# Pooling mixer of an encoder trunk: turned input from memory, row factors by a product with ones, pooled product in the mix banks

## The chip, the cores and the metric

The kernel runs on one core of one Trainium2 chip. The metric is the device time of one execution in microseconds. The core has the matrix engine TensorE (PE in the profile), VectorE (DVE), ScalarE (ACT), GpSimd (POOL) and the queue of SyncE (SP), which only issues transfers here.

## What is computed

One layer (DEPTH is 1) over 2048 rows of a prompt and 512 rows of a sample, each row 1024 wide, all in float32. Cut to what matters:

```python
def rms_norm(x, g):
    y = xf * lax.rsqrt(jnp.mean(xf * xf, axis=-1, keepdims=True) + EPS)
    return y * g

def pool_mixer(h, w, scale):                  # windows 2, 4, 8, 16 rows, 256 channels each
    mean = (take(cs, t + win // 2) - take(cs, t - win // 2)) / cnt
    d = stack(mean - h)                       # per group of 256 channels
    return einsum('bsgc,gce->bsge', d, w) * scale

x = x + pool_mixer(rms_norm(x, norm_mix_g), pool_w, pool_scale)
x = x + sqrelu_mlp(rms_norm(x, norm_mlp_g), w_up, w_down)     # 1024 -> 4096 -> 1024
return rms_norm(x, final_norm_g)
```

## The kernel before

The 2560 rows are five groups of 512 rows. A group goes through the MLP in eight steps (`PAIRS`), so there are 40 steps `n`, with `g = n // 8` and `s = n % 8`. A step has four up tiles (`up_tile`: 24 matmuls of 512 columns each) and the seven products of a Strassen scheme for the down projection (`product`, P1, P5, P6, P3, P4, P7, P2 in this order, 12 matmuls of 512 columns each) of the step before. Each float32 operand is split into a high and a low part (`*_hi`, `*_lo`): ScalarE makes the high part, VectorE the low one. The products go into a ring of two bank pairs (`ring_ps`, turn numbers in `TURN`); VectorE adds each pair into `m_acc` (`evict`). In the steps of group 0 the parts of the down weights are made as well (`split_w`, `sum_w` on VectorE, `w_slot`) and stored; later groups load them again.

While group `g` is in the MLP, the pooling of group `g + 1` is done beside it. In step `s` = 2 (`STATS_STEP`) its rows are loaded to `xr`, ScalarE sums squares (`row_stats`), and GpSimd makes the factor of each row, `rs_x`. In each of the steps 3 to 6 one window `w` of 256 channels is done (16 times in all). ScalarE scales the rows (`norm_rows`, in the step before). TensorE turns them, 8 transposes at the start of the step (`turn_window`) and 2 for the rows beyond the group's ends after the second product (`turn_halos`), into the two banks of `mix_ps`. ScalarE copies them to `ht`. GpSimd sums neighbours in `w + 1` levels (`window_sums`), VectorE subtracts the rows themselves, ScalarE and VectorE split (`dt_hi`, `dt_lo`), and TensorE multiplies by the pooling weights (`pool_out`, 24 matmuls of 256 columns, in two halves, each a turn of the ring). VectorE adds that to `xr` (`add_pooled`).

The order on each engine is written out by hand, engine by engine, in that engine's `step(n)` and `boundary(n)`; semaphores order the engines against each other. What an engine does in an instruction it does not begin before the one ahead of it in this order. The order on TensorE in a window's step is: `turn_window`, up tile 0, P1, P5, `turn_halos`, up tile 1, P6, P3, up tile 2, P4, P7, `pool_out`, up tile 3, P2.

Two places in VectorE's `step(n)` matter below: the part after P7's eviction, which prepares the down weights and activations of the next step (`sum_w`, `split_w`, `split_a`, then `sum_a(n, P5)`, `evict(q0 + P2)`, `split_a(q0 + NP + P5)`); and the end of the step `s` = 2. Group 0 runs from 40 to 394 us of the span, step 2 of it ends at 145.1 us.

Of the kernel before, what the change touches and what calls it, by code (L numbers as in the profile page):

```python
# [6 lines left out]
P = 128  # L7
D = 1024
# [15 lines left out]
TURNS = CT + 1  # L24
# [57 lines left out]
def ring_turns():  # L82

    turns, at = {}, 0
    for n in range(STEPS + 1):
        for k in range(NP if n > 0 else 0):
            turns[NP * (n - 1) + k] = at
            at += 1
            if k == P7 and n < STEPS and pooled_window(n) is not None:
                for half in range(2):  # L90
                    turns[(*pooled_window(n), half)] = at
                    at += 1
    return turns
# [23 lines left out]
def build(nc, x, halos, w_up, w_down, pool_w, pool_scale, g_mix, g_mlp, g_fin, ends, bands, ident_in,  # L117
# [8 lines left out]
    with ctx:  # L126
# [69 lines left out]

        junk = dt_hi[:, :, :].rearrange("p c t -> p (c t)")
# [88 lines left out]
        p4_begun = sem("p4_begun")  # L286
        first_full = sem("first_full")
# [21 lines left out]
        xw_done = sem("xw_done")  # L309
        x_turned = sem("x_turned")  # L310
        ht_done = sem("ht_done")
# [27 lines left out]
        def window_sums(engine, eng, w, ht, room, done_sem, done):  # L339
            src = ht  # L340
# [16 lines left out]
        def _(sp):  # L357
# [38 lines left out]
            def load_halos(m):  # L396
                if m > 1:
                    sp.wait_ge(xw_done, NORMS * WINDOWS * (m - 1))
                sp.dma_start(xh[:, :], halos[m]).then_inc(halo_in, 16)

            def load_pool_w(m, w):
                before = (m, w - 1) if w > 0 else (m - 1, WINDOWS - 1)
                if (*before, 1) in TURN:
                    sp.wait_ge(ring_full, TURN[(*before, 1)] + 1)
# [33 lines left out]
            def step(n):  # L438
# [3 lines left out]
                if mixes and s == STATS_STEP:  # L442
# [4 lines left out]
                    load_ends(g + 1)  # L447
                    load_pool_w(g + 1, 0)
# [32 lines left out]
        def _(act):  # L481
# [932 lines left out]
```

## Time and profile before

| | before |
|---|---|
| median of 3 runs | 1790.6 us (1790.18 to 1791.56) |
| the profiled execution | 1790.22 us, its span 1788.4 us |
| granted clock, mean share | 0.996 |
| PE busy | 1756.3 us (98%) |
| DVE, ACT, POOL busy | 1122.7 (63%), 761.4 (43%), 158.7 us (9%) |
| DMA | 432.67 MB, mean 242 GB/s |

A time in a row of the trace is counted from the start of the span. "Busy" merges overlapping instructions: matmuls overlap, so the spacing of their starts says more than their durations.

### The profile page before, as it was taken

To read this page: it belongs to the slowest core of one execution; us is meant where nothing else is said; L and a number is where in the kernel's file an instruction comes from. 1 tells how busy PE (TensorE), PEld (TensorE's weight loads), DVE (VectorE), ACT (ScalarE), POOL (GpSimd) and SP (SyncE) were. 2 spreads that over 40 slices of the span, in tenths; PEclk is the share of its full clock that TensorE was granted. 3 is DMA by queue.
4 is the path that set the end of the run, shared out by engine and by line. 5 is a ranking of instruction groups with operands and counts; after the bars stand their busy time and mean duration, and the time that the engine had idled before them with its cause. 6 is when DMAs were issued, how large, how long until landed. Compare 5 with 4: busy or idle time off the path is not lost.

```text
span 1788.4 us, 20968 instructions
## 1 busy us (share of the span) xinstructions
PE 1756.3 (98%) x8156; PEld 1461.8 (82%) x8156; DVE 1122.7 (63%) x1178; ACT 761.4 (43%) x1186; POOL 158.7 (9%) x139
## 2 busy tenths in 40 slices
PE   8999999999999999999999999999999999999996
PEld 8888887778888888888888888888888888888885
DVE  6678888786555564765555647645556575445447
ACT  6556554554343335344333344343333543233232
POOL 4000112001001120010011200000112010000001
PEclk9999999999999999999999999999999999999998
DMA  7597766668856665668666555776665657666654
GB/s 266 218 348 281 265 252 242 245 263 326 307 212 224 223 224 212 247 242 295 243 223 223 213 212 204 280 295 223 224 224 212 235 205 273 240 223 239 233 202 163
DMA packets 80902, 432.67 MB, mean 242 GB/s; under 512 B 8860, under 2 KB 10780, under 8 KB 42916
## 3 DMA queue, kind: packets, MB, share of 16 engines
q1 hardware_dynamic: 57764, 347.44, 52.6%
q10 hardware_dynamic: 23040, 83.90, 13.8%
q8 instruction: 65, 1.06, 0.2%
q14 instruction: 33, 0.27, 0.0%
HBM read 360.00 MB, written 71.30 MB: 241 GB/s over the span
## 4 chain that ended last, share of the span: by engine, by line
PE 89%; DVE 6%; ACT 1%; DMA 1%; issue 1%; POOL 1%; ACTq 0%; SPq 0%; POOLq 0%; DVEq 0%
PE up_ps L1169 16%; PE up_ps L1171 16%; PE up_ps L1170 16%; PE ring_ps L1188 13%; PE ring_ps L1190 13%; PE ring_ps L1189 13%; DVE m_acc L832 1%; PE ring_ps L1213 1%; DVE w_slot L765 1%; PE ring_ps L1215 1%; PE ring_ps L1214 1%; DVE a_slot L773 1%; PE mix_ps L1198 1%; DVE wu_lo L756 1%; DMA wd_raw<-w_down 1%
## 5 line engine op out<-in xcount | busy, mean ns | idle before, releaser
L756 DVE TENSOR_TENSOR wu_lo<-wu_raw,wu_hi 128x1024 fp32r<-128x1024 f32 x158 | 195.8, 1239 | 579.7 <-ACT wu_hi L496 579.7
L1169 PE MATMUL up_ps<-h_hi,wu_hi 128*128 128x512 f32 x1280 | 501.4, 392 | 0.6 <-DVE h_lo L897 0.6
L1171 PE MATMUL up_ps<-h_hi,wu_lo 128*128 128x512 f32 x1280 | 498.5, 389 | 0.0
L1170 PE MATMUL up_ps<-h_lo,wu_hi 128*128 128x512 f32 x1280 | 498.5, 389 | 0.0
L533 ACT ACTIVATE a_raw<-up_ps 128x512 f32<-128x512 f32 x160 | 95.3, 596 | 509.0 <-PE up_ps L1171 509.0
L832 DVE TENSOR_TENSOR m_acc<-ring_ps,m_acc 128x1024 f32<-128x1024 f32 x245 | 298.6, 1219 | 18.8 <-PE ring_ps L1190 18.4
L1188 PE MATMUL ring_ps<-w_slot,a_slot 128*128 128x512 f32 x760 | 296.8, 391 | 1.1 <-DVE m_acc L832 1.1
L1190 PE MATMUL ring_ps<-w_slot,a_slot 128*128 128x512 f32 x760 | 295.9, 389 | 0.0
L1189 PE MATMUL ring_ps<-w_slot,a_slot 128*128 128x512 f32 x760 | 295.7, 389 | 0.0
L1171 PEld LDWEIGHTS up_ps<-h_hi,wu_lo 128*128 128x128 f32 x1280 | 240.2, 188 | 50.5
L1169 PEld LDWEIGHTS up_ps<-h_hi,wu_hi 128*128 128x128 f32 x1280 | 240.3, 188 | 49.4 <-DVE h_lo L897 1.2
L1170 PEld LDWEIGHTS up_ps<-h_lo,wu_hi 128*128 128x128 f32 x1280 | 240.4, 188 | 48.3
L525 ACT CAST a_slot<-s_sum 128x512 fp32r<-128x512 f32 x160 | 99.4, 621 | 278.4 <-PE ring_ps L1190 98.5
L1188 PEld LDWEIGHTS ring_ps<-w_slot,a_slot 128*128 128x128 f32 x760 | 142.6, 188 | 31.1 <-issue 1.5
L1190 PEld LDWEIGHTS ring_ps<-w_slot,a_slot 128*128 128x128 f32 x760 | 142.6, 188 | 29.9
L1189 PEld LDWEIGHTS ring_ps<-w_slot,a_slot 128*128 128x128 f32 x760 | 142.7, 188 | 29.2
L496 ACT CAST wu_hi<-wu_raw 128x1024 fp32r<-128x1024 f32 x160 | 165.4, 1034 | 0.0
L1188 PE MATMUL ring_ps<-w_more,a_slot 128*128 128x512 f32 x360 | 140.6, 391 | 0.1
L1190 PE MATMUL ring_ps<-w_more,a_slot 128*128 128x512 f32 x360 | 140.2, 389 | 0.0
L1189 PE MATMUL ring_ps<-w_more,a_slot 128*128 128x512 f32 x360 | 140.1, 389 | 0.0
L773 DVE TENSOR_TENSOR a_slot<-s_sum,a_slot 128x512 fp32r<-128x512 f32 x160 | 134.1, 838 | 3.4 <-ACT a_slot L525 3.4
L525 ACT CAST a_slot<-a_raw 128x512 fp32r<-128x512 f32 x120 | 74.5, 621 | 104.6 <-PE ring_ps L1190 104.5
(136 smaller groups left out, 1642.2 us busy)
## 6 DMA issues: line engine op xcount, KB each, us to landing
w_slot<-w_cache SPq DMA_DIRECT2D x134, 1024.0 KB, 5.1
w_more<-w_cache SPq DMA_DIRECT2D x90, 1024.0 KB, 5.1
wu_raw<-w_up ACTq DMA_DIRECT2D x160, 512.0 KB, 3.2
w_cache<-w_slot SPq DMA_DIRECT2D x56, 1024.0 KB, 4.9
wd_raw<-w_down SPq DMA_DIRECT2D x16, 1024.0 KB, 8.7
xr<-x SPq DMA_DIRECT2D x20, 512.0 KB, 7.6
out<-m_acc SPq DMA_DIRECT2D x20, 512.0 KB, 5.6
pw_slot<-pw_cache SPq DMA_DIRECT2D x16, 512.0 KB, 4.3
```

The source lines that it names most:

```text
L496: nc.scalar.copy(wu_hi[:, u % FT, :, :], wu_raw[:, u % FT, :, :]).then_inc(wu_hi_done, 1)
L525: nc.scalar.copy(a_slot[:, q % A_SLOTS, 0, :, :], a_source(q)).then_inc(a_hi_done, 1)
L533: nc.scalar.activation(a, up_ps[:, u % FT, :], ACT.Relu).then_inc(relu_done, 1)
L756: nc.vector.tensor_tensor(wu_lo[:, u % FT, :, :], wu_raw[:, u % FT, :, :], wu_hi[:, u % FT, :, :].bitcast(f32), ALU.subtract).then_inc(wu_ ...
L773: nc.vector.tensor_tensor(a_slot[:, i, 1, :, :], a_source(q), a_slot[:, i, 0, :, :].bitcast(f32), ALU.subtract).then_inc(a_lo_done, 1)
L832: nc.vector.tensor_tensor(dst, src, dst, ALU.add).then_inc(ring_read, 1)
L1169: nc.tensor.matmul(o, hi, h2_hi[:, d, :], start=(d == 0), stop=False)
L1170: nc.tensor.matmul(o, hi, h2_lo[:, d, :], start=False, stop=False)
L1171: last = nc.tensor.matmul(o, lo, h2_hi[:, d, :], start=False, stop=(d == DT - 1))
L1188: nc.tensor.matmul(dst, a_hi, hi, start=(k == 0), stop=False)
L1189: nc.tensor.matmul(dst, a_hi, lo, start=False, stop=False)
L1190: last = nc.tensor.matmul(dst, a_lo, hi, start=False, stop=(k == 1))
```

## The change

- The input is given a second time, laid out with channels on partitions and with the rows beyond each group's ends (`x_turned`). Two slots `xt` take one window's channels each, by a transfer (`load_turned`, 128x1056 floats). The ten transposes of a window, the scaling in `norm_rows` and the copies to `ht` go.
- The row factors are spread over the partitions once a group. At the end of the step `s` = 2 VectorE sets a tile of ones and a tile with the factors on the diagonal (`set_diag`). At the start of step 3 TensorE multiplies them (`spread_rs`, four products of 128 columns and one of 16, in float32), and ScalarE copies the result to `rs_b` (`keep_rs`). GpSimd multiplies each slot by it, two instructions of 528 elements a window, ahead of the sums.
- The sums of window `w + 1` no longer wait for the transposes of the next step: they wait for the slot, for `rs_b`, and for `dt_lo` of window `w`.
- `pool_out` writes to the two banks of `mix_ps`, in one piece, and stands after up tile 3, behind which only P2 is left. `add_pooled` is one instruction, after the eviction of P2.
- On VectorE the window's subtraction and split stand after the eviction of P7; on ScalarE `split_pooled` stands after `split_a(q0 + 6)`.

```diff
             def load_halos(m):
                 if m > 1:
-                    sp.wait_ge(xw_done, NORMS * WINDOWS * (m - 1))
+                    sp.wait_ge(rs_spread, SPREADS * (m - 1))
+            def load_turned(m, w):
+                v = WINDOWS * (m - 1) + w
+                if v >= 2:
+                    sp.wait_ge(diff_done, v - 1)
+                sp.dma_start(xt[:, w % 2, :, :], x_turned[m - 1, w]).then_inc(xt_in[w % 2], 16)
...
                     load_ends(g + 1)
+                    load_turned(g + 1, 0)
+                    load_turned(g + 1, 1)
                     load_pool_w(g + 1, 0)
...
                 if mixes and WINDOW_STEP <= s < WINDOW_STEP + WINDOWS - 1:
                     load_pool_w(g + 1, s - WINDOW_STEP + 1)
+                if mixes and WINDOW_STEP <= s < WINDOW_STEP + WINDOWS - 2:
+                    load_turned(g + 1, s - WINDOW_STEP + 2)
...
+            def keep_rs(m):
+                act.wait_ge(rs_spread, SPREADS * m)
+                if m > 1:
+                    act.wait_ge(xt_scaled, CT * WINDOWS * (m - 1))
+                nc.scalar.copy(rs_b[:, HALO:HALO + GT], mix_ps[:, 0, :]).then_inc(rs_b_done, 1)
+                nc.scalar.copy(rs_b[:, 0:HALO], mix_ps[:, 1, 0:HALO]).then_inc(rs_b_done, 1)
+                nc.scalar.copy(rs_b[:, HALO + GT:HT], mix_ps[:, 1, HALO:2 * HALO]).then_inc(rs_b_done, 1)
...
             def add_pooled(m, w):
-                c = slice(w * WC, (w + 1) * WC)
-                for half in range(2):
-                    r = TURN[(m, w, half)]
-                    rows = xr[:, 2 * half:2 * half + 2, c]
-                    dve.wait_ge(ring_full, r + 1)
-                    nc.vector.tensor_tensor(rows, ring_pair(r)[:, :, 0:WC], rows, ALU.add).then_inc(ring_read, 1)
+                rows = xr[:, :, w * WC:(w + 1) * WC]
+                dve.wait_ge(pool_full, WINDOWS * (m - 1) + w + 1)
+                nc.vector.tensor_tensor(rows, mix_ps[:, :, :].rearrange("p b (i c) -> p (b i) c", c=WC), rows,
+                                        ALU.add).then_inc(pool_read, 1)
+
+            def set_diag(m):
+                dve.wait_ge(rs_x_done, m)
+                if m > 1:
+                    dve.wait_ge(rs_spread, SPREADS * (m - 1))
+                nc.vector.memset(ones, 1.0).then_inc(diag_done, 1)
+                nc.vector.tensor_tensor(rs_diag[:, 0:GT].rearrange("p (j t) -> p j t", t=P),
+                                        ident[:, :].unsqueeze(1).to_broadcast([P, TT, P]),
+                                        rs_x[:, 0:TT].unsqueeze(2).to_broadcast([P, TT, P]),
+                                        ALU.mult).then_inc(diag_done, 1)
+                nc.vector.tensor_scalar(rs_diag[:, GT:GT + 2 * HALO], ident[:, 0:2 * HALO], rs_x[:, TT:NORMS], None,
+                                        ALU.mult).then_inc(diag_done, 1)
...
-                if windows:
-                    subtract_own(g + 1, w)
-                    split_pooled(g + 1, w)
                 split_wu(4 * n + 4)
                 if n > 0:
                     evict(q0 + P4)
                     split_a(q0 + P2)
                     evict(q0 + P7)
+                if windows:
+                    subtract_own(g + 1, w)
+                    split_pooled(g + 1, w)
                 sum_w(n, P5)
                 split_w(q0 + NP + P1)
                 split_a(q0 + NP + P1)
-                if windows:
-                    add_pooled(g + 1, w)
                 split_w(q0 + NP + P5)
...
                 if n > 0:
                     evict(q0 + P2)
+                if windows:
+                    add_pooled(g + 1, w)
+                if g < LAST and s == STATS_STEP:
+                    set_diag(g + 1)
                 split_a(q0 + NP + P5)
...
             def next_sums(m, w):
+                v = WINDOWS * (m - 1) + w
+                slot = xt[:, w % 2, :, :]
+                pool.wait_ge(xt_in[w % 2], 16 * (v // 2 + 1))
+                pool.wait_ge(rs_b_done, 3 * m)
+                for c in range(CT):
+                    nc.gpsimd.tensor_tensor(slot[:, c, :], slot[:, c, :], rs_b[:, :], ALU.mult).then_inc(xt_scaled, 1)
                 pool.wait_ge(ends_in, 16 * m)
-                pool.wait_ge(ht_done, TURNS * (WINDOWS * (m - 1) + w + 1))
-                window_sums(nc.gpsimd, pool, w, ht, sums, summed,
+                if v > 0:
+                    pool.wait_ge(dt_lo_done, v)
+                pool.wait_ge(xt_scaled, CT * (v + 1))
+                window_sums(nc.gpsimd, pool, w, slot, sums, summed,
                             SUM_STEPS[WINDOWS] * (m - 1) + SUM_STEPS[w])
...
+            def spread_rs(m):
+                pe.wait_ge(diag_done, 3 * m)
+                for j in range(TT):
+                    nc.tensor.matmul(mix_ps[:, 0, j * P:(j + 1) * P], ones, rs_diag[:, j * P:(j + 1) * P],
+                                     start=True, stop=True).then_inc(rs_spread, 1)
+                nc.tensor.matmul(mix_ps[:, 1, 0:2 * HALO], ones, rs_diag[:, GT:GT + 2 * HALO],
+                                 start=True, stop=True).then_inc(rs_spread, 1)
...
-                if windows:
-                    turn_window(g + 1, w)
+                if g < LAST and n % PAIRS == WINDOW_STEP:
+                    spread_rs(g + 1)
                 up_tile(4 * n)
                 product(q0 + 0)
                 product(q0 + 1)
-                if windows:
-                    turn_halos(g + 1, w)
...
                 product(q0 + 4)
                 product(q0 + 5)
+                up_tile(4 * n + 3)
                 if windows:
                     pool_out(g + 1, w)
-                up_tile(4 * n + 3)
                 product(q0 + 6)
```

On VectorE, at the end of step 2 of group 0, the order before is this (`m_acc<-ring_ps` is the eviction of P2, `a_slot` the low part of the activations for P5, `wu_lo` and `s_sum` are for the next step):

```order
L756 TENSOR_TENSOR wu_lo<-wu_raw,wu_hi 128x1024
L809 TENSOR_TENSOR s_sum<-a_raw 128x512
L832 TENSOR_TENSOR m_acc<-ring_ps,m_acc 128x1024
L773 TENSOR_TENSOR a_slot<-s_sum,a_slot 128x512
L812 TENSOR_TENSOR s_sum<-s_sum,a_raw 128x512
```

The changed kernel has in the same place (`halo_room` holds the ones and the diagonals):

```order
L746 TENSOR_TENSOR wu_lo<-wu_raw,wu_hi 128x1024
L799 TENSOR_TENSOR s_sum<-a_raw 128x512
L822 TENSOR_TENSOR m_acc<-ring_ps,m_acc 128x1024
L870 MEMSET halo_room 128x128
L871 TENSOR_TENSOR halo_room<-ident,rs_x 128x512
L875 TENSOR_SCALAR halo_room<-ident,rs_x 128x16
L763 TENSOR_TENSOR a_slot<-s_sum,a_slot 128x512
L802 TENSOR_TENSOR s_sum<-s_sum,a_raw 128x512
```

Three instructions are put in, behind the eviction of the step's last product.

On TensorE, where step 3 of group 0 begins, the last matmuls of P2 and the first of up tile 0 had the eight transposes between them:

```order
L1189 MATMUL ring_ps<-w_slot,a_slot 128x512
L1190 MATMUL ring_ps<-w_slot,a_slot 128x512
L1198 MATMUL mix_ps<-ident,xw 128x128 x8
L1169 MATMUL up_ps<-h_hi,wu_hi 128x512
L1170 MATMUL up_ps<-h_lo,wu_hi 128x512
```

Now they have the products with ones there, which wait for the three instructions above:

```order
L1201 MATMUL ring_ps<-w_slot,a_slot 128x512
L1202 MATMUL ring_ps<-w_slot,a_slot 128x512
L1229 MATMUL mix_ps<-halo_room 128x128 x4
L1231 MATMUL mix_ps<-halo_room 128x16
L1181 MATMUL up_ps<-h_hi,wu_hi 128x512
L1182 MATMUL up_ps<-h_lo,wu_hi 128x512
```

In the steps 4, 5 and 6 nothing stands between the last product of a step and up tile 0.

On VectorE, in a window's step of group 0, this follows the eviction of P7 in the changed kernel (`sums` is the subtraction, `dt_lo` the split, then the weights and activations of the next step):

```order
L822 TENSOR_TENSOR m_acc<-ring_ps,m_acc 128x1024
L888 SCALAR_TENSOR_TENSOR sums<-sums,xt 128x2x512
L893 TENSOR_TENSOR dt_lo<-sums,dt_hi 128x1024
L775 TENSOR_TENSOR t_sum<-wd_raw 128x1024
L755 TENSOR_TENSOR w_slot<-wd_raw,w_slot 128x1024
L763 TENSOR_TENSOR a_slot<-a_raw,a_slot 128x512
L755 TENSOR_TENSOR w_slot<-t_sum,w_slot 128x1024
L779 TENSOR_TENSOR wd_raw<-wd_raw 128x2x512
L783 TENSOR_TENSOR t_sum<-wd_raw,t_sum 128x1024
L746 TENSOR_TENSOR wu_lo<-wu_raw,wu_hi 128x1024
L799 TENSOR_TENSOR s_sum<-a_raw 128x512
L822 TENSOR_TENSOR m_acc<-ring_ps,m_acc 128x1024
```

The rows from `t_sum` on are those of before; the first two behind the eviction stood three evictions and splits earlier, and GpSimd's sums for the next window are now released by the `dt_lo` row.

## Rows read from the trace of the kernel before

**Rows 1.** The page: span, busy time and instructions of each engine.
```profile
span 1788.4 us, 20968 instructions
PE 1756.3 (98%) x8156; PEld 1461.8 (82%) x8156; DVE 1122.7 (63%) x1178; ACT 761.4 (43%) x1186; POOL 158.7 (9%) x139
```

**Rows 2.** Waits of TensorE: total us, times, longest us.
```profile
PE ring_ps L1213 <- DVE m_acc L832: 5.7, 2, 4.0
```

**Rows 3.** Timeline of TensorE round a window's transposes: start us, us, instruction.
```profile
144.88 0.39 PE L1190 MATMUL ring_ps<-w_slot,a_slot 128*128 128x512 f32 x1
145.11 1.03 PE L1198 MATMUL mix_ps<-ident,xw 128*128 128x128 f32 x8
...
146.22 0.40 PE L1170 MATMUL up_ps<-h_lo,wu_hi 128*128 128x512 f32 x1
...
156.89 0.38 PE L1205 MATMUL mix_ps<-ident,xw 128*128 128x128 f32 x2
...
157.34 0.39 PE L1170 MATMUL up_ps<-h_lo,wu_hi 128*128 128x512 f32 x1
```

**Rows 4.** Groups by line and shape on TensorE: count, busy us, mean ns.
```profile
L1198 PE MATMUL mix_ps<-ident,xw 128*128 128x128 f32 x128 | 16.5, 272 | 0.0
...
L1256 PE MATMUL mix_ps<-band_x,first_x 128*128 128x112 f32 x12 | 1.9, 278 | 0.0
```

**Rows 5.** Timeline of TensorE, first pooled matmul and first of the next tile.
```profile
887.75 0.28 PE L1213 MATMUL ring_ps<-pw_slot,dt_hi 128*128 128x256 f32 x1
...
890.76 0.40 PE L1169 MATMUL up_ps<-h_hi,wu_hi 128*128 128x512 f32 x1
```

**Rows 6.** Timeline of TensorE at its two waits in group 0.
```profile
271.21 0.36 PE L1213 MATMUL ring_ps<-pw_slot,dt_hi 128*128 128x256 f32 x1 [1.74 <-DVE m_acc L832]
...
316.15 0.39 PE L1190 MATMUL ring_ps<-w_slot,a_slot 128*128 128x512 f32 x1
320.49 0.52 PE L1213 MATMUL ring_ps<-pw_slot,dt_hi 128*128 128x256 f32 x1 [3.96 <-DVE m_acc L832]
```

**Rows 7.** Busy time by stretch (PE, PEld, DVE, ACT, POOL), granted clock, DMA.
```profile
320.60:323.90 3.30, 3.30 (x16) 3.30 (x17) 3.30 (x4) 1.09 (x2) 0.00 (x0) 0.50 1.02 428
```

**Rows 8.** Timelines of VectorE and TensorE where a step 2 ends (groups 0, 2).
```profile
149.40 0.68 DVE L773 TENSOR_TENSOR a_slot<-s_sum,a_slot 128x512 fp32r<-128x512 f32 x1
...
853.93 1.03 PE L1198 MATMUL mix_ps<-ident,xw 128*128 128x128 f32 x8
...
856.52 0.68 DVE L773 TENSOR_TENSOR a_slot<-s_sum,a_slot 128x512 fp32r<-128x512 f32 x1
...
14.97 0.27 DVE L926 MEMSET xw<- 128x256 f32 x1
```

**Rows 9.** Timelines of VectorE and GpSimd during the sums of window 3, group 0.
```profile
297.23 2.13 DVE L773 TENSOR_TENSOR a_slot<-s_sum,a_slot 128x512 fp32r<-128x512 f32 x1
...
301.62 2.94 DVE L765 TENSOR_TENSOR w_slot<-t_sum,w_slot 128x1024 fp32r<-128x1024 f32 x1
304.48 3.42 DVE L756 TENSOR_TENSOR wu_lo<-wu_raw,wu_hi 128x1024 fp32r<-128x1024 f32 x1
...
296.86 1.94 POOL L347 TENSOR_TENSOR sums<-ht 128x1052 f32<-128x1052 f32 x1 [39.33 <-ACT ht L569]
298.88 7.94 POOL L347 TENSOR_TENSOR sums<-sums 128x1048 f32<-128x1048 f32 x3
```

**Rows 10.** Timelines of TensorE and VectorE where P3 ends, group 2, step 3.
```profile
876.87 0.39 PE L1169 MATMUL up_ps<-h_hi,wu_hi 128*128 128x512 f32 x1
...
877.07 1.22 DVE L832 TENSOR_TENSOR m_acc<-ring_ps,m_acc 128x1024 f32<-128x1024 f32 x1 [0.25 <-PE ring_ps L1190]
878.21 0.68 DVE L773 TENSOR_TENSOR a_slot<-s_sum,a_slot 128x512 fp32r<-128x512 f32 x1
878.81 1.22 DVE L887 SCALAR_TENSOR_TENSOR sums<-sums,ht 128x1024 f32<-128x1024 f32 x1
881.14 1.22 DVE L892 TENSOR_TENSOR dt_lo<-sums,dt_hi 128x1024 fp32r<-128x1024 f32 x1 [1.12 <-ACT dt_hi L573]
```

More of the change, by code:

```diff
@@ L23 @@
 RING = 4
-TURNS = CT + 1
+SPREADS = TT + 1
 FP = 4
@@ L195, in build @@
         rs_f = sb("rs_f", [P, TT])
+        xh = halo_room[0:2 * HALO, :]
+        rs_diag = halo_room[:, 0:GT + 2 * HALO]
+        ones = halo_room[:, D - P:D]
         junk = dt_hi[:, :, :].rearrange("p c t -> p (c t)")
@@ L308, in build @@
         rs_x_done = sem("rs_x_done")
-        xw_done = sem("xw_done")
-        x_turned = sem("x_turned")
-        ht_done = sem("ht_done")
+        diag_done = sem("diag_done")
+        rs_spread = sem("rs_spread")
+        rs_b_done = sem("rs_b_done")
+        xt_in = [sem(f"xt_in{i}") for i in range(2)]
+        xt_scaled = sem("xt_scaled")
         summed = sem("summed")
@@ L669, in step @@
                 windows = mixes and 0 <= w < WINDOWS
-                if windows:
-                    keep_turned(g + 1, w)
+                if mixes and s == WINDOW_STEP:
+                    keep_rs(g + 1)
                 activate(4 * n)
@@ L999, in step @@
                 split_a(q0 + NP + P1)
-                if windows:
-                    add_pooled(g + 1, w)
                 split_w(q0 + NP + P5)
@@ L1222, in pool_out @@
                 pe.wait_ge(pw_slot_in, 16 * (v + 1))
-                for half in range(2):
-                    r = TURN[(m, w, half)]
-                    pe.wait_ge(ring_read, r - 1)
-                    for i in range(2):
-                        pool_tile(2 * half + i, ring_pair(r)[:, i, 0:WC], (dt_hi, dt_lo),
-                                  (pw_slot[:, 0, :, :], pw_slot[:, 1, :, :]), ring_full if i == 1 else None)
+                if v % WINDOWS > 0:
+                    pe.wait_ge(pool_read, v)
+                for j in range(TT):
+                    pool_tile(j, mix_ps[:, j // 2, j % 2 * WC:(j % 2 + 1) * WC], (dt_hi, dt_lo),
+                              (pw_slot[:, 0, :, :], pw_slot[:, 1, :, :]), pool_full if j == TT - 1 else None)
+            def spread_rs(m):
+                pe.wait_ge(diag_done, 3 * m)
+                for j in range(TT):
+                    nc.tensor.matmul(mix_ps[:, 0, j * P:(j + 1) * P], ones, rs_diag[:, j * P:(j + 1) * P],
+                                     start=True, stop=True).then_inc(rs_spread, 1)
+                nc.tensor.matmul(mix_ps[:, 1, 0:2 * HALO], ones, rs_diag[:, GT:GT + 2 * HALO],
+                                 start=True, stop=True).then_inc(rs_spread, 1)
             def transpose(m, d):
@@ L1300, in step @@
                 product(q0 + 1)
-                if windows:
-                    turn_halos(g + 1, w)
                 up_tile(4 * n + 1)
@@ L1387 @@
             halos.append(np.concatenate([rows[at:at + HALO], rows[at + HALO + GT:at + HT]]))
+            turned.append(rows[at:at + HT].T.reshape(WINDOWS, CT, P, HT).transpose(0, 2, 1, 3))
     arrays = {
```

80 lines of the change are left out of this document (19 added, 61 removed).

## Prediction, made before the result was known

> **What bounds the kernel now.** I read the page first, then the waits and the timeline of TensorE, then VectorE and GpSimd at the places where the change acts. TensorE is busy in 1756.3 of 1788.4 us [rows 1]. From 876.87 to 887.75 are an up tile and two products, 48 matmuls of 512 columns in 10.88 us, one every 0.2267 [rows 5, 10]; 7200 of them (3840 in up tiles, 3360 in products) make 1632 us. So time is won only by work or waits that leave TensorE. Its only waits inside a window's step are two of 5.7 us in all, both in group 0, at the pooled product, for an eviction by VectorE [rows 2]. Elsewhere VectorE and ScalarE may change their work freely until they are late for TensorE. Group 0 is the place where VectorE can be late, since it splits the down weights there.
>
> **What the change removes.**
> (a) The transposes. Eight of them push the second up matmul from one spacing (0.23) to 1.11 us behind their start: 0.88. Two for the rows beyond the ends take 157.34 - 156.89 - 0.23 = 0.22 [rows 3]. There are 128 of the first kind [rows 4], so 16 windows: 16 x 1.10 = 17.6 us.
> (b) The two old waits. They stem from the half of the pooled product that needs a ring pair, and from VectorE being late in mid-step. From 316.15 to 320.49 are 4.34 us instead of 0.23; the other wait shows 1.74 us idle [rows 6], plus the 0.16 by which a matmul's tail of 0.39 outlasts the spacing. Together 4.1 + 1.9 = 6.0 us. The new place needs no ring pair.
> (c) The stop between the halves. 24 pooled matmuls took 3.01 us [rows 5]; at half the spacing and a little, 0.12, they need 2.87. 16 x 0.14 = 2.2 us (bounds 0 and 3).
> (d) After the 3.96 us of idle the clock was granted at half for 3.3 us (0.50, the 1.2 GHz level) [rows 7], with TensorE busy throughout. It did half the work in that time: 1.6 us.
> Sum 27.4 us off.
>
> **What it adds on TensorE.**
> (e) The spread. It is in float32, for which the trace has two records a matmul: the program has six of 112 columns into `mix_ps`, the trace 12 [rows 4]. So ten records a group. Transposes of 128 columns cost 0.88 / 8 = 0.11 each [rows 3]; the float32 records' busy time over their number is 0.16, tails included [rows 4]. At 0.11 each and 0.1 for the next tile's start: 1.2 a group, 4.8 us for four (bounds 4.4 and 6.8).
>
> **The new wait, at the start of step 3.** (f) `spread_rs` is ahead of up tile 0 in TensorE's order, and everything on TensorE queues behind it. It waits for `set_diag`, which VectorE has behind the eviction of P2, the very product that TensorE does last before it. In group 2 TensorE began step 3 at 853.93; VectorE's eviction of P2 let the next instruction begin at 856.52 [rows 8], because it stands behind the low part of the next weights and a sum of activations that need up tile 3. There the three new instructions come: a memset of 128 (at most the 0.27 of 256 elements [rows 8]; I take 0.15), a product of 512 elements (0.68, the row of that size) and one of 16 (0.1). They end near 857.4; with 0.1 for the semaphore TensorE goes on at 857.5: 3.6 us of wait, in groups 1 to 3 alike. In group 0 VectorE runs without a pause there and is later: 149.40 for the same point, against 145.11 on TensorE [rows 3, 8]; 150.4 - 145.1 = 5.3 us. Together 3 x 3.6 + 5.3 = 16.1 us (bounds 14.5 and 17.5). I see no cover: no matmul is left between P2 and the spread.
>
> **Is the pooled product in time?** P7 now ends where up tile 3 starts, call it E. What follows a product's end is to be seen behind P3 in group 2, which ends at 876.87: VectorE takes it 0.20 later and its next instruction 1.34 later (878.21), from the subtraction to the split, with ScalarE's part between them, are 881.14 - 878.81 = 2.33, and the split takes 1.22 [rows 10]. So `dt_lo` is done at E + 4.9. Up tile 3 takes 24 x 0.2267 = 5.4. So it is in time by 0.4 us (0.1 of it the semaphore). I cost it at nothing; what covers it is up tile 3, and each 0.1 us beyond costs 1.6 us over 16 windows.
>
> **The sums in group 0.** (g) The sums for window w + 1 now run on GpSimd from the moment `dt_lo` is done, T = E + 4.9. In the rows of before, GpSimd's sums and VectorE's instructions with both inputs in SBUF alternate: an activations' low part of 0.68 [rows 8] took 2.13, a weights' one took 2.94, the next 3.42, and in the 10.7 us from 297.2 to 307.9 VectorE got four instructions done [rows 9]. The last three levels took 7.94 with 0.48 of one of VectorE's instructions and the whole of two (0.68 and 1.22) inside, so 5.56 net, which I read as 1.65 to 1.75 a level and 2.25 for the last; the ends I put at 0.45. The eviction is not held.
> After T VectorE has, for the next step: the weights' sum, P1's split of weights (1.14 each, counted start to start), P1's of activations (0.6), P5's split, two sums, the next up weights (1.14 each), the sum of activations (0.6); then the eviction of P2 and `add_pooled` (1.14 each), and last P5's split of activations (0.6). TensorE begins P5 at T + 14.2: up tile 3 to E + 5.4, pooled product 2.9, P2 2.7, up tile 0 5.4, P1 2.7.
> Walked in turns, the last item ends, counted from T: after window 1's two levels at 15.7, after window 2's three at 17.5, after window 3's four at 19.2; with no sums beside it (window 3's own step) at 11.0. The waits are 1.5, 3.4 and 5.0: 9.9 us, in the steps 4, 5 and 6 of group 0. Bounds: nothing for the first and a microsecond less for each of the others, 6; or 14, where GpSimd's two new products of 528 elements fall in as well. I price these at 1.0 (half of 1.94 for 1052 elements [rows 9]); their slot's transfer is issued behind a store that waits for P5's split, so I put them after this stretch for windows 2 and 3.
> In groups 1 to 3 the weights' work is absent, and the same walk ends at T + 10.8, 3.4 us early. What is new on VectorE in mid-step is less than before.
> (h) The clock. Idle of 3.96 us was followed by half clock, 1.74 us was not [rows 6, 7]. I take 1.6 us for each of the two waits of 5, 3.2 us; the four others, with about 3.4 us idle or less, at nothing (bounds 0, and 4.8 more for those of 3.6).
> The Trainium skill (TensorE: Matmul & The Clock Gate, Part 1) says that the clock falls once an idle stretch fills one of the monitor's own periods, so the place of the idle time counts beside its length. By that rule each of the long waits may or may not be followed by half clock; it is a rival below.
> The rest costs nothing: 16 transfers of 0.54 MB beside 432 MB, in steps where a weights' load is issued some 20 us ahead of its use; ScalarE loses about 50 us of work (five scalings and three copies a window) but TensorE did not wait for it.
>
> **The sum.** Off 27.4; on 4.8 + 16.1 + 9.9 + 3.2 = 34.0; net 6.6 us slower. Against the profiled execution, 1790.2, that is 1796.8; its median is 1790.6, so 1797.
>
> **Rivals.**
> 1. VectorE is not late in group 0. For it: the sums leave mid-step, where they cost the old 6.0 us, and my turns are a hand walk through one stretch of four instructions. Against: group 0's VectorE never paused round step ends, and the new place has 8 us of its work before a due time. Then (g) is 0 and (h) 1.6: 27.4 - 22.5 = 4.9 us faster, 1785.7. It ends on the faster side once (g) and (h) together are below 3 us. 0.13.
> 2. The gains and the new waits cancel: (g) about 5 us, as much as VectorE's lateness cost before, and one fall of the clock. 27.4 - 4.8 - 16.1 - 5 - 1.6: within 0.2 us of before, 1790 (1787 to 1794). 0.22.
> 3. The spread does not wait, because VectorE reaches `set_diag` sooner than the rows of step 2 show. Nothing in the change brings the eviction of P2 forward, it waits for a product that ends just then. 27.4 - 4.8 - 9.9 - 1.6 = 11 us faster, 1779. 0.03.
> 4. Worse by the same mechanisms: the clock falls after the waits of 3.6 too (4.8), or the pooled product is late by some tenths in 16 windows (0.2 us too late is 3.2), or GpSimd's products fall into the late stretch (4). 1801 to 1806. 0.12. The skill's rule on the idle stretch's place, named above, would give this where all stretches fit, and spare the 3.2 of (h) where none does.
> 5. The forecast, 1794 to 1801: 0.50.
>
> **How the numbers follow.** What a measurement of this kernel can tell from no change is about 0.2%, 3.6 us. Faster by more: rivals 1 and 3, 0.16. Within: rival 2, 0.22. Slower by more: the forecast and rival 4, 0.62. The range leaves out rival 3, the better half of 1 and the worse half of 4: 1786 to 1803. The forecast alone has 1794 to 1801.
>
> **What would show it.** Transposes gone and ten records a group of `mix_ps<-halo_room`, about 1.1 us each time: (a), (e). Four waits of TensorE at that line for VectorE's diagonal, three near 3.6 us and one near 5.3: (f). Waits at the first matmul of P5 in steps 4 to 6 of group 0, growing with the window, with VectorE's SBUF instructions stretched beside GpSimd's sums: (g). No wait at the pooled product, and its 24 matmuls in 2.9 us: (b), (c). Stretches of clock 0.50 right after the two longest waits: (h). The prediction is wrong in its sign if (g) and (h) come to less than 6.5 us.

## The result, and the profile after

The changed kernel takes 1805.5 us (median of 6 runs, 1804.7 to 1808.5) against 1790.6 for the kernel before in the same comparison: a ratio of 1.0085, 95% interval 1.0072 to 1.0098. It is slower by 15 us. The forecast was 1797 with a range of 1786 to 1803, so the sign was right and the size too small, outside the range.

The head of the page of the changed kernel answers to [rows 1]:

```profile
span 1804.3 us, 20677 instructions
PE 1751.9 (97%) x8036; PEld 1456.8 (81%) x8036; DVE 1119.7 (62%) x1173; ACT 712.9 (40%) x1070; POOL 209.9 (12%) x171
```

TensorE is busy for 4.4 us less in a span that is 15.9 us longer, so it is idle for 20.3 us more. Its busy time isn't all useful either: matmuls at half clock take longer and count as busy. Its waits in total (us, times, longest) say for whom it was idle; they answer to [rows 2]:

```profile
PE mix_ps L1229 <- DVE halo_room L875: 18.5, 4, 8.3
PE ring_ps L1200 <- DVE a_slot L763: 6.5, 3, 4.1
PE mix_ps L1241 <- DVE h_lo L898: 4.7, 5, 2.9
```

The old wait at the pooled product is gone. The first row is the spread, which waits for VectorE's diagonal tiles once a group. The second is at the first matmul of a product in group 0, for a part of the activations that VectorE splits: P3 in step 4 (0.55) and P5 in steps 5 and 6. The third stands in the boundaries between groups. Of the first kind, the waits of group 0 and of group 2 look so in TensorE's timeline; the last shown is the longest at P5, in step 6:

```profile
145.76 0.39 PE L1202 MATMUL ring_ps<-w_slot,a_slot 128*128 128x512 f32 x1
154.43 0.79 PE L1229 MATMUL mix_ps<-halo_room 128*128 128x128 f32 x2 [8.28 <-DVE halo_room L875]
...
867.57 0.39 PE L1202 MATMUL ring_ps<-w_slot,a_slot 128*128 128x512 f32 x1
871.35 0.38 PE L1229 MATMUL mix_ps<-halo_room 128*128 128x128 f32 x1 [3.39 <-DVE halo_room L875]
...
301.97 0.39 PE L1202 MATMUL ring_ps<-w_slot,a_slot 128*128 128x512 f32 x1
306.46 0.79 PE L1200 MATMUL ring_ps<-w_slot,a_slot 128*128 128x512 f32 x1 [4.11 <-DVE a_slot L763]
```

Counted from the start of P2's last matmul, less the spacing of 0.23, TensorE loses 8.44 us in group 0 and 3.55 in groups 1 to 3: 19.1 in all. The last matmul shown is 0.79 long, twice the 0.39 of its neighbours. The stretches behind show why (us, then busy time of PE, PEld, DVE, ACT and POOL with instructions, the granted clock, DMA); they answer to [rows 7]:

```profile
154.50:159.00 4.50, 4.50 (x16) 4.02 (x17) 3.52 (x4) 0.72 (x3) 1.35 (x1) 0.50 0.32 135
258.30:261.60 3.30, 3.30 (x9) 2.63 (x8) 3.27 (x2) 0.74 (x1) 2.59 (x2) 0.50 0.58 236
306.00:309.30 3.30, 2.84 (x7) 2.26 (x8) 3.23 (x4) 2.73 (x4) 0.00 (x0) 0.50 0.62 199
391.40:394.70 3.30, 3.30 (x12) 2.61 (x11) 3.30 (x5) 2.47 (x4) 0.00 (x0) 0.50 0.19 79
521.10:524.40 3.30, 3.12 (x12) 2.96 (x13) 1.41 (x3) 0.72 (x3) 0.00 (x0) 0.50 0.33 132
524.50:527.70 3.20, 3.20 (x9) 2.52 (x8) 0.00 (x0) 0.00 (x0) 3.03 (x3) 0.50 0.00 0
872.70:876.00 3.30, 3.30 (x9) 2.53 (x9) 0.00 (x0) 0.70 (x3) 2.46 (x2) 0.50 0.01 5
1220.80:1224.10 3.30, 3.30 (x12) 2.72 (x11) 0.36 (x1) 0.72 (x3) 1.74 (x2) 0.50 0.05 20
```

The granted clock was at half (0.50, the 1.2 GHz level) behind all four waits of the spread, behind two of P5's and once in the first boundary. The kernel before had one such stretch, apart from the one at the very end of either kernel.

Every step still ends with P2, so the loss can be read by steps. The next table is worked out from the traces: the length of a step, from the start of the last matmul of its P2 to that of the next step's, in us. "g0 s3" is step 3 of group 0, and "g1 s0" the first boundary. The experiments' rows are explained below.

```
                  g0 s3   g0 s4   g0 s5   g0 s6   g1 s0   g1 s3   g2 s3   g3 s3
before            45.09   45.33   47.06   50.55   39.99   45.01   45.04   44.99
after             55.63   44.96   47.46   49.43   40.98   51.58   50.05   50.07
e1_diag_early     47.22   44.96   46.71   49.67   40.91   44.81   44.81   44.81
e2_fill_wait      54.91   44.97   47.47   50.73   40.30   48.50   48.47   48.50
e3_turned_later   53.09   44.95   46.70   49.71   40.64   50.07   50.07   50.11
e4_sums_late      55.67   43.71   45.58   45.51   40.57   50.10   50.10   51.51
e7_sums_cut       55.53   44.97   43.67   43.67   40.91   51.23   50.05   50.10
e8_spread_late    49.54   44.95   47.48   50.79   40.97   44.81   44.81   44.81
e6_fill_doses     55.87   44.97   46.68   49.68   40.86   48.45   48.47   51.53
e10_fill_all      53.34   44.95   46.69   49.69   39.57   48.47   48.49   48.47
e5_three          44.81   43.71   45.58   45.51   40.72   44.81   44.81   44.81
e9_sums_parted    44.81   43.71   43.67   44.07   42.31   44.81   44.81   44.81
```

The other window steps of groups 1 to 3 take 43.67 in each changed kernel and 45.0 before; their steps outside the windows are the same within 0.1. So an undisturbed window step is 43.67, and 44.81 with the spread.

### The profile page after: what moved, and what is told of

Same layout as the page of the kernel before. It is cut to its first block, busy times and chain, and to the rows that moved or that the text cites. A ratio compares the mean times of both kernels' runs of the same rounds, so it can differ in the third digit from the quotient of the medians.

```text
span 1804.3 us, 20677 instructions
## 1 busy us (share of the span) xinstructions
PE 1751.9 (97%) x8036; PEld 1456.8 (81%) x8036; DVE 1119.7 (62%) x1173; ACT 712.9 (40%) x1070; POOL 209.9 (12%) x171
## 4 chain that ended last, share of the span: by engine, by line
PE 84%; DVE 8%; issue 2%; ACT 2%; DMA 2%; POOL 1%; ACTq 0%; SPq 0%; POOLq 0%; DVEq 0%
PE up_ps L1181 15%; PE up_ps L1182 15%; PE up_ps L1183 15%; PE ring_ps L1200 12%; PE ring_ps L1202 12%; PE ring_ps L1201 12%; DVE m_acc L822 2%; DVE w_slot L755 1%; DVE a_slot L763 1%; DVE wu_lo L746 1%; DMA w_cache<-w_slot 1%; DMA wd_raw<-w_down 1%; PE mix_ps L1209 1%; PE mix_ps L1211 1%; PE mix_ps L1210 1%
## 5 line engine op out<-in xcount | busy, mean ns | idle before, releaser
L746 DVE TENSOR_TENSOR wu_lo<-wu_raw,wu_hi 128x1024 fp32r<-128x1024 f32 x158 | 205.9, 1303 | 594.1 <-ACT wu_hi L502 594.1
L763 DVE TENSOR_TENSOR a_slot<-s_sum,a_slot 128x512 fp32r<-128x512 f32 x160 | 110.5, 690 | 3.4 <-ACT a_slot L531 3.4
```

Source lines behind the costliest of these rows:

```text
L746: nc.vector.tensor_tensor(wu_lo[:, u % FT, :, :], wu_raw[:, u % FT, :, :], wu_hi[:, u % FT, :, :].bitcast(f32), ALU.subtract).then_inc(wu_ ...
L763: nc.vector.tensor_tensor(a_slot[:, i, 1, :, :], a_source(q), a_slot[:, i, 0, :, :].bitcast(f32), ALU.subtract).then_inc(a_lo_done, 1)
```

## The experiments

Theory 1: the spread's wait, and the clock that falls behind it, carry the loss. Theory 2: group 0's extra 3 us of that wait come from the transfers of the slices. Theory 3: GpSimd's sums hold VectorE, and so the products P5 of steps 4 to 6, in group 0. The rivals stand in each expectation. Ratios are to the kernel before, in the same comparison, with 95% intervals.

### e1_diag_early

```diff
                     evict(q0 + P7)
+                if g < LAST and s == STATS_STEP:
+                    set_diag(g + 1)
                 if windows:
...
                     add_pooled(g + 1, w)
-                if g < LAST and s == STATS_STEP:
-                    set_diag(g + 1)
                 split_a(q0 + NP + P5)
```

> VectorE's three instructions for the spread (ones, the four diagonal tiles, the halo's) stand behind P7's eviction of step 2, not behind P2's; the row factors are there by then (138.35 + 1.17 in group 0, 856.03 + 1.18 in group 2). Theory 1, the spread's wait and the half clock behind it carry the loss: the four waits of 8.44 and 3 x 3.55 (19.1) go, and what step 3 is longer by beyond its wait (2.2, 3.1, 1.6 and 1.6 in groups 0 to 3, together 8.5) goes too: about 1778, so faster than the kernel before by 12, with no granted clock of 0.50 at 149, 521, 873 and 1221. Rival A, VectorE is full in group 0, whatever the order: there 4 or more of the 8.4 come back as a wait of the product P5 in step 3 for its operand (it was ready at 154.96), with half clock behind it: 1784 to 1787. Rival B, the clock's fall has another cause than the waits: only the 19.1 goes, 1786.5, and the stretches at 0.50 stay.

Measured: 1779.3 us, ratio 0.9938 (0.9923 to 0.9953). One order of three small instructions turns a kernel that is slower than before into a faster one. VectorE is past its three by 144.1, and TensorE runs on (timeline of TensorE, group 0):

```profile
144.82 0.39 PE L1202 MATMUL ring_ps<-w_slot,a_slot 128*128 128x512 f32 x1
145.05 1.05 PE L1229 MATMUL mix_ps<-halo_room 128*128 128x128 f32 x8
...
146.08 0.48 PE L1181 MATMUL up_ps<-h_hi,wu_hi 128*128 128x512 f32 x1
```

The gain is 26.2, near theory 1's 27.6. What is missing is mainly a wait in step 3 of group 0 (1.73 idle at 167.51), rival A in small: the step takes 47.22, not 44.81. It stands at P3, two products behind the P5 that the expectation names. Rival B falls, since no stretch at half clock is left behind the spread.

### e8_spread_late

```diff
                 if g < LAST and n % PAIRS == WINDOW_STEP:
+                    up_tile(4 * n)
                     spread_rs(g + 1)
-                up_tile(4 * n)
+                else:
+                    up_tile(4 * n)
```

and the same exchange of `keep_rs` and `activate(4 * n)` on ScalarE.

> VectorE's order stays as in the changed kernel; on TensorE the spread stands behind the first tile of step 3 (24 matmuls of 0.216, so 5.2 later), and ScalarE's copy of it behind the activation of that tile. Theory 1 (only the place of the spread against its operands counts): no wait in groups 1 to 3, 3.2 of 8.44 left in group 0: 5.2 + 3 x 3.55 + the half clock of groups 1 to 3 (6.3) + some of group 0's 2.2: 1781 to 1784. Rival (the wait moves: ScalarE's three copies, which wait for the spread, now stand between the activation and the split of the operands and hold P1 or P5): the same waits of 1 or more come back at the products of step 3, 1786 or more.

Measured: 1782.9 us, ratio 0.9949 (0.9935 to 0.9964). Moving the consumer does what moving the producer did: 44.81 in groups 1 to 3, and in group 0 a rest of 2.85 idle with 1.7 lost to half clock behind it. The rival's wait behind ScalarE's copies didn't come.

### e2_fill_wait, e6_fill_doses, e10_fill_all: what the clock takes

```diff
             def spread_rs(m):
+                if m > 1:
+                    pe.wait_ge(pool_read, WINDOWS * (m - 1))
+                for _ in range(28):
+                    nc.tensor.transpose(mix_ps[:, 1, 0:P], ident[:, :], ident[:, :])
                 pe.wait_ge(diag_done, 3 * m)
```

The count is 28 in each group; in the second kernel 0, 24, 16 and 8 for groups 0 to 3; in the third 68 in group 0 and 28 in the others. The wait stays as long, but TensorE works through part of it.

> Computes the same; 28 transposes of the identity (20 took 2.35 us at full clock, so 28 about 3.3) go to TensorE ahead of the spread's wait, where it stood idle for 3.55 (8.44 in group 0). Theory 1 (the idle stretch halves the clock, which costs 3.1, 1.6 and 1.6 in groups 1 to 3 beyond the wait): waits under 0.4 stay in groups 1 to 3 and no stretch at 0.50 behind them, 6.3 gained; in group 0 5.1 idle are left, which still costs the clock: 1799, and 1797 if the clock holds there too. Rival (the clock's price is small and the extra length of step 3 is the spread itself): the time stays within 1.5 of 1805.5.

> As the kernel with 28 transposes ahead of the spread, but with 0, 24, 16 and 8 in groups 0 to 3, so that idle stretches of about 0.7, 1.7 and 2.6 are left of the 3.55 in groups 1, 2 and 3; the length of step 3 shows the clock's part alone, since filling gives back no wait (it is 48.5 where the clock holds and 50.05 to 51.6 where it fell). Theory 1 (any idle stretch of 3 or more lowers the clock, shorter ones some times): group 1 at 48.5, group 2 at 48.5 or, as at P5 in group 0 (a stretch of 2.0 was followed by 0.50), at 50.1, group 3 at 50.1; in all 1800 to 1804. Rival (the length of the wait has no part in it, only its place in time): 50.05 to 51.6 in all three groups, 1805.5.

> As the kernel with 28 transposes ahead of the spread, with 68 (about 8.0) in group 0, so nearly no idle stretch is left there. Theory 1 (clock): step 3 of group 0 falls from 55.63 by 2.2 to about 53.4, groups 1 to 3 as with 28 (48.5 each): together 8.4 to 8.5 is what the clock took behind the spread's waits, 1797. Rival (in group 0 VectorE's lateness at P5 would follow even at full clock): step 3 of group 0 stays at 54.9 or more, 1798.8.

Measured: 1798.8 (ratio 1.0047, 1.0032 to 1.0062), 1801.6 (1.0056, 1.0039 to 1.0073) and 1796.5 (1.0031, 1.0020 to 1.0042). Useless work made the kernel faster by 9 us at most. By the table the part behind the spread's waits is 2.29 + 3.11 + 1.56 + 1.60 = 8.6 us in the third kernel. The remaining difference from 44.81, 3.7 in each of groups 1 to 3, is the wait itself.

The doses part the cases. The timeline of TensorE in the kernel with doses, where 24, 16 and 8 transposes were put:

```profile
516.61 2.78 PE L1230 MATMUL mix_ps<-ident 128*128 128x128 f32 x24
520.16 1.16 PE L1233 MATMUL mix_ps<-halo_room 128*128 128x128 f32 x8 [0.77 <-DVE halo_room L875]
...
863.56 1.91 PE L1230 MATMUL mix_ps<-ident 128*128 128x128 f32 x16
867.11 1.16 PE L1233 MATMUL mix_ps<-halo_room 128*128 128x128 f32 x8 [1.64 <-DVE halo_room L875]
...
1210.50 1.03 PE L1230 MATMUL mix_ps<-ident 128*128 128x128 f32 x8
1214.05 2.08 PE L1233 MATMUL mix_ps<-halo_room 128*128 128x128 f32 x8 [2.51 <-DVE halo_room L875]
```

and the granted clock behind each (columns as above):

```profile
521.30:524.50 3.20, 3.20 (x17) 2.69 (x16) 0.13 (x1) 0.72 (x3) 2.15 (x2) 1.00 0.05 20
868.30:871.50 3.20, 3.20 (x15) 2.66 (x15) 0.07 (x1) 0.72 (x3) 2.20 (x2) 1.00 0.09 36
1213.80:1217.10 3.30, 3.05 (x12) 2.96 (x13) 1.48 (x4) 0.70 (x3) 0.00 (x0) 0.50 0.31 122
1217.20:1220.40 3.20, 3.20 (x9) 2.52 (x8) 0.00 (x0) 0.00 (x0) 2.97 (x3) 0.50 0.00 0
```

Idle stretches of 0.77 and 1.64 left the clock at full; 2.51 was followed by half clock in both stretches shown, and step 3 took 51.53, 3.1 over the 48.45. The expectation had 50.1 there: a fall costs about 1.6, or twice that when half clock lasts twice as long. The rival, that the wait's length has no part in it, has these three stretches against it. They don't show that length alone decides; the last section has stretches that speak against that.

### e3_turned_later

```diff
                     load_ends(g + 1)
-                    load_turned(g + 1, 0)
-                    load_turned(g + 1, 1)
-                    load_pool_w(g + 1, 0)
                 store_w(q0 + 3)
...
                 load_w(q0 + 10)
+                if mixes and s == STATS_STEP:
+                    load_turned(g + 1, 0)
+                    load_turned(g + 1, 1)
+                    load_pool_w(g + 1, 0)
```

> The two transfers of the transposed slices and that of the pooled weights are issued at the end of step 2's queue, not ahead of the stores. Theory 2 (the burst of 115.4 to 116.9 held the stores, so the split of the weights waited 3.45 for a landing, and the row statistics and VectorE behind it came late): group 0's wait of the spread falls from 8.4 to 5.2 to 5.6, and the time by 3 to 4.5 (with part of the half clock): 1801 to 1802.5. The first boundary is not touched by it. Rival (VectorE's own work makes group 0's wait long): within 1 of 1805.5, the wait still over 7.5. A danger is that the slices now land behind 157.7 and hold GpSimd: no matter before the first pooled product's 190.

Measured: 1801.3 us, ratio 1.0066 (1.0050 to 1.0083). The spread's longest wait is now 5.1 us, near the 5.3 forecast. In ScalarE's timeline the changed kernel's split of a weights' operand waited for a store's landing, and the row statistics (L544) queued behind it:

```profile
130.93 1.05 ACT L519 CAST w_slot<-wd_raw 128x1024 fp32r<-128x1024 f32 x1 [3.45 <-DMA w_cache<-w_slot]
131.89 1.05 ACT L544 ACTIVATE dt_hi<-xr 128x1024 fp32r<-128x1024 f32 x1
```

With the transfers moved the same instruction has no wait, as in the kernel before:

```profile
126.83 1.05 ACT L520 CAST w_slot<-wd_raw 128x1024 fp32r<-128x1024 f32 x1
127.78 1.05 ACT L545 ACTIVATE dt_hi<-xr 128x1024 fp32r<-128x1024 f32 x1
```

So theory 2 holds. Step 3 of group 0 is shorter by 2.5, less than the 3.2 of the wait, because more of the half clock stood behind the shorter wait. It lasted to 156.5 and the spread began at 150.3, so TensorE worked through 6.2 us of it; in the changed kernel through 4.8 (154.4 to 159.2).

```profile
150.40:156.40 6.00, 6.00 (x19) 5.19 (x20) 3.51 (x4) 0.72 (x3) 2.86 (x2) 0.50 1.03 416
```

At half speed that is 3.1 lost against 2.4, and 3.2 - 0.7 = 2.5. TensorE has a fourth wait for VectorE's split of activations here (7.0 us in four, for 6.5 in three), but it stands at P3 of step 5, where this kernel's clock did not fall.

### e4_sums_late and e7_sums_cut: GpSimd's sums in group 0

```diff
                     pool.wait_ge(dt_lo_done, v)
+                    if m == 1:
+                        pool.wait_ge(a_lo_done, NP * (WINDOW_STEP + w - 1) + P5 + 1)
```

The second kernel has the old release, and leaves work out instead: in `window_sums`, `n = HALO` for windows 2 and 3 of group 0.

> In group 0 alone GpSimd's sums of windows 1 to 3 wait until VectorE has split the operand of P5 at the end of a step. Theory 3 (the sums, released by dt_lo in the midst of VectorE's fullest stretch, stretch its operations of 0.7 and 1.2 to 2.4 and 2.9, and so hold P5): the waits of 0.7, 2.0 and 4.3 at P5 in steps 4 to 6 go, with the half clock at 258.21 and 305.99 (1.7 each): up to 10 gained, 1796 to 1798. Rival (VectorE is nearly full there, so the same sums in the next 12 us press on its splits of weights and evictions, 0.6 to 1.2 us longer each): the waits come back some 10 us later, in the ring or at P3 and P7, and the time is within 3 of 1805.5 or above it.

> Leaves work out: in group 0 the neighbour sums of windows 2 and 3 cover 8 columns a level, not over 1030, so their seven operations fall from 2.5 to 2.8 each to a few tenths. Theory 3 (GpSimd's sums hold VectorE): the waits at P5 in steps 5 and 6 (2.0 and 4.3) and the half clock at 258.21 and 305.99 go, that of step 4 (0.7) stays: step 5 falls from 47.46 to about 43.7 and step 6 from 49.43 to about 43.7, 9 to 9.5 gained, 1796. Rival (VectorE is late there by its own work, or by ScalarE's): both steps stay over 45.5, under 5 gained.

Measured: 1797.4 us (ratio 1.0039, 1.0024 to 1.0054) and 1795.8 (1.0024, 1.0015 to 1.0033). With the sums cut, steps 5 and 6 fall to 43.67 exactly, so all of the 9.5 us there came from them. With the sums only later P5's waits are gone and 1.9 us stays in each of the two steps, at P3 in step 5 and at P6 and P3 in step 6: the rival is right to that extent. (The wait of 0.7 in step 4 that the first expectation puts at P5 is at P3.) VectorE's timeline in the changed kernel, during window 3's sums, answers to [rows 9]:

```profile
288.96 2.96 DVE L755 TENSOR_TENSOR w_slot<-wd_raw,w_slot 128x1024 fp32r<-128x1024 f32 x1
291.85 2.42 DVE L763 TENSOR_TENSOR a_slot<-a_raw,a_slot 128x512 fp32r<-128x512 f32 x1
294.19 2.94 DVE L755 TENSOR_TENSOR w_slot<-t_sum,w_slot 128x1024 fp32r<-128x1024 f32 x1
297.05 3.42 DVE L779 TENSOR_TENSOR wd_raw<-wd_raw 128x1024 f32<-128x1024 f32 x1
```

and GpSimd's beside it:

```profile
288.05 2.80 POOL L343 TENSOR_TENSOR sums<-xt 128x1052 f32<-128x1052 f32 x1 [27.16 <-DVE dt_lo L893]
290.92 8.47 POOL L343 TENSOR_TENSOR sums<-sums 128x1048 f32<-128x1048 f32 x3
```

VectorE's four instructions take 11.5 us, as long as GpSimd's four levels; free of GpSimd they take 4.0 (starts of such instructions lie 0.60 and 1.14 apart).

### e5_three and e9_sums_parted: what can be had

The first has the edits of e1, e3 and e4. The second adds a stop in the sums of windows 2 and 3 in group 0, ahead of their last two levels:

```diff
+                def halt(level):
+                    if m == 1 and w >= 2 and level == w - 1:
+                        pool.wait_ge(a_lo_done, NP * (WINDOW_STEP + w - 1) + P7 + 1)
```

> The three edits together: the spread's operands made earlier, the transfers of the slices behind the stores, group 0's sums behind the split for P5. Theory: they act on different waits, so they add: 1779.3 less the 7.0 that the late sums gave in steps 4 to 6 of group 0, less 0.5 to 2 of the wait of 2.1 at P5 that is left in step 3, less 0.4 to 0.7 at the boundary: 1769.5 to 1772, a ratio of 0.989 to the kernel before. Rival (group 0's VectorE is full, and the 9 us that the first edit gives there only move its lateness on): the waits at P5 come back, 1776 or more.

> The kernel with the three edits, and in group 0 the last two levels of the sums of windows 2 and 3 wait until VectorE has split the operand of P7, some 19 us behind P5's. In the kernel with the three edits the waits of 1.57 (step 5) and about 1.6 in two pieces (step 6) that are left stand behind VectorE's operations stretched to 2.8 to 3.0 next to the sums; behind P7's split VectorE idles 2.8. Theory 3: with half the sums moved there the lateness falls under what the products bear, both waits go or halve: 1.5 to 3.8 gained on 1769.8, 1766 to 1768. Rival (the product P5 of the next step, or the subtraction of the own rows, now waits for the last level): a wait before the pooled product and the same time or more, 1770 to 1773.

Measured: 1769.8 us (ratio 0.9876, 0.9861 to 0.9891) and 1767.5 us (0.9867, 0.9849 to 0.9884), both faster than either kernel of the case. The edits act on separate waits: those of e1 and e3 on step 3, that of e4 on steps 4 to 6. In the last kernel the parts of the sums stand apart (GpSimd's timeline):

```profile
283.39 1.96 POOL L344 TENSOR_TENSOR sums<-xt 128x1052 f32<-128x1052 f32 x1 [15.37 <-DVE a_slot L765]
285.43 2.80 POOL L344 TENSOR_TENSOR sums<-sums 128x1048 f32<-128x1048 f32 x1
303.51 5.26 POOL L344 TENSOR_TENSOR sums<-sums 128x1040 f32<-128x1040 f32 x2 [15.29 <-DVE a_slot L765]
```

The waits that the three edits had left at P3 and P6 are gone; TensorE's list of waits begins with those of a boundary and of the start:

```profile
PE mix_ps L1248 <- DVE h_lo L900: 5.9, 5, 3.5
PE ring_ps L1256 <- DMA ident<-ident_in: 2.7, 1, 2.7
```

Steps 5 and 6 took 3.35 less than with the three edits, and the boundary 1.6 more. Step 6 keeps 0.4 over 43.67; TensorE's only stop in it is one before the pooled product, which the rival named, here small.

## Why the forecast was right in sign and wrong in size

By steps, in us of the profiled executions (+ is slower), with the forecast's terms beside them:

- **(a) and (c), transposes and the stop between halves:** forecast -19.8. Sixteen window steps went from 45.0 to 43.67: -21.3.
- **(b) and (d), the old waits and their clock:** forecast -7.6. Over 45.0, group 0's four steps had 0.09 + 0.33 + 2.06 + 5.55 = 8.0: -8.0.
- **(e), the spread:** forecast +4.8; 4 x (44.81 - 43.67) = +4.6.
- **(f), its wait:** forecast +16.1, as 3 x 3.6 and 5.3. The waits are 3 x 3.55 and 8.44, so +19.1. The structure was right: the walk through VectorE's order gave groups 1 to 3 within 0.05 each. Group 0's 5.3 was taken from the place of VectorE in the kernel before; two transfers that the change itself issues ahead of the stores moved ScalarE and VectorE 4 us later there (e3). "16 transfers of 0.54 MB beside 432 MB" cost "nothing" was the wrong step here: the total is small, but two of them stand in the queue ahead of the store that a weights' slot is waiting for. (e3 moved the pooled weights' transfer with them; the kernel before has that one ahead of the same stores, without the delay.)
- **(g) with its part of (h), P5 in steps 4 to 6:** forecast 9.9 + 1.6 = +11.5. Over 43.67 these steps have 1.29 + 3.79 + 5.76 = +10.8. The mechanism holds (e7), but the sum agrees in part by luck. By the spacings of the matmuls the waits are 1.2 in step 4 (0.4 at P5, 0.8 at P3), 2.1 in step 5 and 4.3 in step 6: 7.6 for the 9.9 walked. The other 3.2 is half clock behind P5 in steps 5 and 6, two falls, for the one forecast at 1.6; the fall in step 5 came behind 1.87 us of idle, of the kind that (h) put at nothing.
- **(h), the clock behind the spread's waits:** forecast +1.6, for group 0 alone, and the three of 3.6 "at nothing", with 4.8 kept as a bound. Over 44.81, step 3 has 10.82, 6.77, 5.24 and 5.26, together 28.1; less the waits of 19.1 this is +9.0, of which filling the waits shows 8.6 as the clock's. This is the step that failed most: the clock was put at nothing behind the waits of 3.6, and it fell behind each of them.
- **Not forecast:** the first boundary +1.0, the start and step 2 of group 0 +0.9.

Together -21.3 - 8.0 + 4.6 + 19.1 + 10.8 + 9.0 + 1.0 + 0.9 = +16.1, against +15.9 in the spans. Against the forecast's +6.6 that is 9.5 more: 7.4 of clock, 3.0 of wait in group 0 and 1.9 not seen, less 0.7 by which (g) with its clock was cheaper and 2.1 by which (a) to (e) came out better.

Why was the clock mis-sized? The two points of [rows 6, 7], half clock after 3.96 us of idle and none after 1.74, leave open where between them the fall begins. I put it above 3.4 idle for no reason that a row gave, and three of the spread's four waits lay between, at 3.39, as did P5's 1.87 in step 5. Rival 4 named this case, and its 1801 to 1806 holds the measured 1805.5, but it had 0.12 and 4.8 us: it priced a fall at 1.6 throughout, while half clock lasted twice as long in group 1 (3.1) and cost 2.3 in group 0. Its other two conditions, a pooled product that is late and GpSimd's products in the late stretch, weren't what made the number.

The pooled product was in time, as walked: no wait in the list, and its matmuls at 0.118 spacing. The rivals: 1 and 2 (VectorE not late, or half as late) fall with e7's 9.5 us; 3 (no wait of the spread) is false for this kernel. Its price of 11 us faster is near what e1 then got, 11.3 (1790.6 - 1779.3), in part by luck: (a) to (e) came out 2.1 better, and step 3 of group 0 kept 2.4 over 44.81.

**Open.** Why the first boundary varies from 39.57 to 42.31 among these kernels wasn't pursued; half clock is part of it where there is a fall, and the transfer of the weights that VectorE waits for there was not tried. The small differences at the start (103.2 to 104.7 up to the end of P2 in step 1, in kernels with the same start) are of unknown cause.

## What to carry to other kernels

When an instruction waits for another engine, ask where its operand could have been made at the earliest: here the row factors were ready 10.6 us before TensorE began to wait in group 2 (867.80 against 856.03 + 1.18) and 6.5 in group 0, while VectorE's three instructions stood behind the last eviction; in groups 1 to 3 the wait was in the written order alone. Price an idle stretch of TensorE, where it sets the time, as the idle time plus half of the half-clock stretch that may follow; here stretches from 1.77 to 3.51 us went either way, so that the second term is a risk and not a certainty. For a new transfer look at the one that is queued behind it and who waits for that, not at the total of bytes.

## What the runs showed of the hardware

**The same idle, two clocks.** TensorE's wait at P5 in step 5 of group 0 is 1.87 us in both e1_diag_early and e2_fill_wait, with the same instructions round it:

```profile
247.42 0.50 PE L1200 MATMUL ring_ps<-w_slot,a_slot 128*128 128x512 f32 x1 [1.87 <-DVE a_slot L763]
```

```profile
254.52 0.50 PE L1200 MATMUL ring_ps<-w_slot,a_slot 128*128 128x512 f32 x1 [1.87 <-DVE a_slot L763]
```

Behind it the clock was granted in full in the first and at half in the second:

```profile
247.60:250.80 3.20, 3.20 (x15) 2.58 (x16) 3.17 (x3) 2.10 (x3) 3.06 (x2) 1.00 0.56 169
```

```profile
255.30:258.50 3.20, 3.20 (x9) 2.51 (x8) 3.17 (x2) 1.49 (x3) 2.46 (x2) 0.51 0.82 334
```

The step took 46.71 in the one and 47.47 in the other. Half clock cost less than its 1.6 there, since the first kernel then waited another 0.5 for VectorE at P3 and the second did not. So an idle stretch of about 2 us may or may not be followed by half clock; 0.77 and 1.64 weren't, 2.51 and the spread's four of 3.39 and more in the changed kernel were.

Longer ones may be spared too. In the first boundary TensorE waited 2.94 us in the changed kernel and 2.54 in e4_sums_late, with half clock behind both, but 2.61 in e3_turned_later and 2.90 in e8_spread_late with full clock behind. In e9_sums_parted the clock stayed up behind 3.51, and fell behind the 1.77 that came ten microseconds later:

```profile
370.04 1.32 PE L1248 MATMUL mix_ps<-ident,x1n 128*128 128x128 f32 x8 [3.51 <-DVE h_lo L900]
...
380.27 1.32 PE L1248 MATMUL mix_ps<-ident,x1n 128*128 128x128 f32 x8 [1.77 <-DVE h_lo L900]
```

```profile
370.00:373.40 3.40, 3.36 (x18) 2.72 (x19) 3.40 (x4) 2.12 (x4) 0.00 (x0) 1.00 0.09 39
382.10:385.40 3.30, 3.30 (x9) 2.58 (x8) 3.30 (x5) 1.15 (x2) 0.00 (x0) 0.50 0.28 119
```

So the length of a stretch alone doesn't settle it in these runs. That the idle's place in time counts beside its length is what the Trainium skill says (TensorE: Matmul & The Clock Gate, Part 1), and these runs agree. By the same part a fall needs a longer idle stretch than 1.87 us; the runs show falls behind that, and the measurement decides.

**GpSimd and VectorE.** Beside GpSimd's sums of window 3 in group 0, VectorE's instructions with both inputs in SBUF take 2.4 to 3.4 us instead of 0.7 and 1.2; an eviction from PSUM beside sums keeps its 1.21 (658.26 in the changed kernel). GpSimd's own level of 1052 elements took 2.80 there. In e9_sums_parted the same level took 1.96, but not because it was alone: it began at 283.39, and VectorE's split that began at 283.46 took 2.96. The Trainium skill (GPSIMD Engine Reference, Key points) says that GpSimd contends with VectorE's instructions that have two SBUF inputs; this trace agrees, and adds the price: 11.5 us for 4.0 of VectorE's work.
